# Picking a pair's tokens out of x by one-hot products in the last experts

## The reference

```python
def expert_choice_ffn(h, w_router, w_gate, w_up, w_down):      # h: 512 x 1024, 16 experts
    cap = CAPACITY_FACTOR * seq // N_EXPERTS                   # 64
    probs = softmax(h @ w_router)
    gate, idx = lax.top_k(transpose(probs), cap)               # each expert chooses its 64 tokens
    xs = h[idx]                                                # 16 x 64 x 1024
    a = xs @ w_gate[e]; u = xs @ w_up[e]                       # 1024 x 2048 each
    y = (silu(a) * u) @ w_down[e] * gate                       # 2048 x 1024
    return segment_sum(y, idx)                                 # added up by token

h2 = rms_norm_2(x, norm2_g)
x = x + expert_choice_ffn(h2, w_router, w_gate, w_up, w_down)
return rms_norm_2(x, final_g)
```

## Time and profile before

| what | us |
|---|---|
| median of 3 runs | 1988.26 (1986.86 to 1988.77) |
| profiled execution, its own time | 1970.76 |
| span of its trace, first to last instruction | 1969.4 |
| PE busy in the span | 1794.5 (91%) |
| DVE busy | 632.2 (32%) |
| ACT busy | 269.0 (14%) |
| POOL busy | 59.6 (3%) |

### The profile page before, as it was taken

How to read it: one execution, slowest core, us unless ns; L and a number is a source line. 1 busy time by engine, 2 the same in 40 slices (tenths; PEclk the granted TensorE clock), 3 DMA queues, 4 the chain that set the end, 5 groups by cost and what they waited for, 6 DMA issues and landing times.

```text
span 1969.4 us, 20545 instructions
## 1 busy us (share of the span) xinstructions
PE 1794.5 (91%) x8838; PEld 854.9 (43%) x8838; DVE 632.2 (32%) x1173; ACT 269.0 (14%) x490; POOL 59.6 (3%) x72
## 2 busy tenths in 40 slices
PE   8999999989999899999989999888888888888886
PEld 4778786533333354577554333222222222232222
DVE  7885453451213267954240111011111011111012
ACT  1251000210000155131010000000000000000001
POOL 0000000042100010000000000000000000000000
PEclk9999999989999999999999999999999999999999
DMA  8412226279999823013659999999999999999996
GB/s 230 146 43 82 90 86 243 101 247 418 425 425 410 307 99 115 25 60 125 267 203 365 427 428 426 429 427 429 427 428 427 428 428 427 428 427 429 427 428 266
DMA packets 88160, 593.04 MB, mean 301 GB/s; under 512 B 24832, under 2 KB 26240, under 8 KB 56832
## 3 DMA queue, kind: packets, MB, share of 16 engines
q1 hardware_dynamic: 79360, 563.24, 69.9%
q0 software_dynamic: 4544, 14.68, 2.1%
q10 hardware_dynamic: 4160, 13.75, 1.8%
HBM read 579.06 MB, written 12.59 MB: 300 GB/s over the span
## 4 chain that ended last, share of the span: by engine, by line
PE 59%; DMA 34%; DVE 4%; issue 1%; ACT 1%; POOL 0%; DVEq 0%; ACTq 0%; SPq 0%
PE ps L253 23%; DMA AR<-in_w_up 15%; PE ps L1399 10%; DMA ring<-in_w_up 7%; DMA AR<-in_w_down 7%; PE ps L2582 7%; PE ps L2608 6%; PE ps L2221 3%; PE ps L827 3%; DMA ring<-in_exp_w_gate 2%; DMA ring<-in_w_down 2%; PE ps L741 2%; PE ps L2116 1%; PE ps L267 1%; PE ps L2563 1%
## 5 line engine op out<-in xcount | busy, mean ns | idle before, releaser
L2722 DVE TENSOR_TENSOR XT<-XT,ps 128x512 f32<-128x512 f32 x128 | 82.0, 684 | 784.1 <-PE ps L2563 784.1
L253 PE MATMUL ps<-AR,ring 128*128 128x256 f32 (+1 forms) x904 | 275.3, 457 | 2.5 <-DVE AR L2412 2.4
L2582 PE MATMUL ps<-ring,AR 128*64 128x512 f32 x1008 | 229.3, 598 | 47.9 <-DMA ring<-in_w_up 31.0
L2582 PE MATMUL ps<-AR 128*64 128x512 f32 x1040 | 235.8, 597 | 31.5 <-DMA AR<-in_w_up 24.7
L1399 PE MATMUL ps<-ring,AR 128*32 128x512 f32 x1536 | 246.7, 593 | 6.1 <-DMA ring<-in_exp_w_gate 4.2
L253 PEld LDWEIGHTS ps<-AR,ring 128*128 128x128 f32 x904 | 171.1, 190 | 96.6 <-issue 77.4
L2582 PEld LDWEIGHTS ps<-ring,AR 128*64 128x64 f32 x1008 | 69.2, 136 | 200.4 <-issue 113.2
L2582 PEld LDWEIGHTS ps<-AR 128*64 128x64 f32 x1040 | 71.9, 137 | 191.5 <-issue 121.2
L253 PE MATMUL ps<-AR 128*128 128x256 f32 (+6 forms) x600 | 123.2, 353 | 7.8 <-DVE AR L1226 3.3
L1399 PE MATMUL ps<-AR 128*32 128x512 f32 x768 | 123.4, 593 | 0.0
L2608 PE MATMUL ps<-ring,AR 128*64 128x512 f32 x496 | 118.4, 626 | 4.7 <-DMA ring<-in_w_down 2.5
(11 more groups left out here) (383 smaller groups left out, 1458.0 us busy)
## 6 DMA issues: line engine op xcount, KB each, us to landing
AR<-in_w_gate SPq DMA_DIRECT2D x33, 2048.0 KB, 35.0
AR<-in_w_down SPq DMA_DIRECT2D x33, 2048.0 KB, 35.4
ring<-in_w_up SPq DMA_DIRECT2D x32, 2048.0 KB, 35.4
AR<-in_w_up SPq DMA_DIRECT2D x32, 2048.0 KB, 35.4
ring<-in_w_gate SPq DMA_DIRECT2D x31, 2048.0 KB, 32.1
ring<-in_w_down SPq DMA_DIRECT2D x31, 2048.0 KB, 35.4
ring<-in_exp_w_gate SPq DMA_DIRECT2D x15, 2048.0 KB, 11.8
ring<-in_w_in SPq DMA_DIRECT2D x14, 2048.0 KB, 10.0
```

Of the source, the lines that this page charges most:

```text
L253: x = PE.matmul(ps, l, r, start=i == 0, stop=i == len(pairs) - 1)
L2582: x = PE.matmul(GU[2 * m + f // 2][64 * (f % 2):64 * (f % 2) + 64, :], XS[n // 2 % 2][:, k * P + 64 * b:k * P + 64 * b + 64], w[:, kk_, f ...
L2722: DV.tensor_tensor(XK[:, o:o + T], XK[:, o:o + T], co_bank(i)[:, :], ALU.add).then_inc(d_co, 1)
```

## The change

- H2E, its four writes, the scaling of the rows (dve_turn splits, dve_rows stays with the first block only), the gathers, pool_choice, the index search and the index columns go.
- The choice keeps only the gate values of the two lists, and takes the 64th largest as the expert's threshold. PE spreads it to all partitions. DVE marks scores above it and equal to it, PE counts the marks by bf16 products with a triangle and with ones, and DVE makes of that a place (slots, 1 to 64, or 0) for each token and expert. Equal scores come behind the larger ones, in the order of tokens.
- For each pair DVE makes a one-hot matrix PICK of 512 tokens by 128 places, each row times the token's reciprocal root (sel). PE multiplies x with it: 8 blocks of 128 columns by 4 blocks of 128 tokens, 32 products of 128x128x128 (picks), and DVE multiplies the result with the norm's gain on its way to XS (gained). The gain (g22d) is loaded as columns.
- The pair's picks are done in the down phase of the pair before, behind its c = 1 and c = 2; those of pair 0 ahead of expert 0 and between its first products.
- cGE comes from one-hots of 128 tokens by 64 places for each block (gates, four operations of DVE), turned by four transposes in the down phase and copied from PSUM by DVE.
- x has to stay as it is until the last picks, so the results are added up in YS (4096 columns), and YS is added to x at expert 14.
- XS, cHE, cHB, cYE and cGE are single.
- The first eleven loads have the buffers 3, 2, 6, 7, 8, 4, 0, 10, 5, 1, 9, then nine go round: 3, 2, 6, 7, 8, 4, 0, 5, 1.

```diff
-        slot += [3, 2, 6, 7, 8, 0, 4, 5, 1, 9, 10]
-        slot += [(3, 2, 6, 7, 8, 0, 1, 9)[i % 8] for i in range(len(loads) - n_ec - 11)]
+        slot += [3, 2, 6, 7, 8, 4, 0, 10, 5, 1, 9]
+        slot += [(3, 2, 6, 7, 8, 4, 0, 5, 1)[i % 9] for i in range(len(loads) - n_ec - 11)]
...
+            SP.wait_ge(s_pp, 182)
+            for n in range(n1, n1 + NX + 1):
                 sp_load(n)
-            sp_load(n_ec + 6)
+            sp_load(n_ec + 7)
 
...
-            for a in range(4):
-                x = PE.transpose(Y5[1 - a // 2][0:16, sl(a % 2, P)], lg[:, a, :], ident)
+            for i in range(2):
+                x = PE.transpose(Y5[1][0:48, sl(i, P)], lg[:, 16 * i:16 * i + 48], ident)
             x.then_inc(s_cp, 1)
-            idle_products(DN, 14)
-
+            idle_products(DN, 11)
+            PE.wait_ge(s_cv, V2_TH)
+            PE.transpose(bank[3][:, 0:16], last_[0:16, 0:1].to_broadcast([16, P]), ident[0:16, 0:16]).then_inc(s_cp, 1)
+            idle_products(DN, 1)
+
+            PE.wait_ge(s_cv, V2_MK)
+            pos = bank[2][:, 0:128].rearrange("p (a n) -> p a n", a=4)
+            for t in range(4):
+                PE.matmul(pos[:, t, :], tri2, marks[:, t, :], start=t == 0, stop=False, skip_group_check=True)
+                if t < 3:
+                    PE.matmul(pos[:, t + 1:4, :], one2, marks[:, t:t + 1, :].to_broadcast([P, 3 - t, 32]), start=False,
+                              stop=False, skip_group_check=True)
+                x = PE.matmul(pos[:, :, 16:32], one2, marks[:, t:t + 1, 0:16].to_broadcast([P, 4, 16]), start=False,
+                              stop=t == 3, skip_group_check=True)
             x.then_inc(s_cp, 1)
+            idle_products(DN, 3)
...
+            def picks(k0, k1, ps):
+
+                for k in range(k0, k1):
+                    c = 256 * (k // 2) + k % 2
+                    x = matmuls(ps[:, sl(k - k0, P)], [(XT[:, a * D + c:a * D + c + 255:2],
+                                                        PICK[:, a, :, :].rearrange("p h s -> p (h s)")) for a in range(4)])
+                x.then_inc(e_tx, 1)
...
-            PE.wait_ge(s_cv, V2_ID)
-            idle_products(DN, 7)
-            rows(0)
+            PE.wait_ge(d_sel, 1)
+            for h in range(2):
+                picks(2 * h, 2 * h + 2, P_BANK[h])
             for n in range(16):
+                s0 = n % 2 * 64
...
+                        if n == 0 and m == 0:
+                            PE.wait_ge(d_xs, c + 1)
+                        elif c == 0 and m == 0:
+                            PE.wait_ge(d_xs, picked(n // 2))
+                            PE.wait_ge(d_he, 2 * n)
...
-                    if c == 1 and (n == 1 or b == 0 and 0 < n < 14):
-                        rows(n // 2 + 1)
+                    elif c < 2:
+                        picks(4 + 2 * c, 6 + 2 * c, P_BANK[2 + c])
...
+                    if c == 0:
+
+                        PE.wait_ge(d_gs, n + 1)
+                        transposes(TR, [GS[:, a, :, :].rearrange("p h s -> p (h s)") for a in range(4)]).then_inc(e_gt, 1)
+                    elif c < 3 and s0 and n < 15:
+                        if c == 1:
+                            PE.wait_ge(d_ge, n + 1)
+                            PE.wait_ge(d_sel, n // 2 + 2)
+                        picks(4 * c - 4, 4 * c, HB[c - 1])
...
+            src = Y5[1]
             for n in range(8):
                 g8 = gat[0:48, sl(n, 8)]
                 DV.max(g8, src[0:48, 0:256]).then_inc(s_dv, dv())
                 DV.wait_ge(s_dv, dv.n)
-                DV.max_index(ixu[0:48, sl(n, 8)].bitcast(U32), g8, src[0:48, 0:256]).then_inc(s_dv, dv())
                 if n < 7:
-                    DV.match_replace(wk[0:48, 0:256], g8, src[0:48, 0:256], -1.0).then_inc(s_dv, dv())
-                DV.wait_ge(s_dv, dv.n)
+                    op(DV.match_replace(wk[0:48, 0:256], g8, src[0:48, 0:256], -1.0))
                 src = wk
...
+            ga_, gb_ = gat[0:16, :], gatb[0:16, :]
+            op(DV.tensor_copy(gb_, gat[32:48, ::-1]))
+            op(DV.tensor_tensor(ga_, ga_, gb_, ALU.max))
+            DV.tensor_reduce(last_[0:16, :], ga_, AX.X, ALU.min).then_inc(s_cv, 1)
+            DV.wait_ge(s_cp, P2_TH)
+            th16 = bank[3][:, 0:16].unsqueeze(1).to_broadcast([P, 4, 16])
+            DV.tensor_tensor(marks[:, :, 0:16], scores, th16, ALU.is_gt)
+            DV.tensor_tensor(marks[:, :, 16:32], scores, th16, ALU.is_equal).then_inc(s_cv, 1)
+            DV.wait_ge(s_cp, P2_PS)
+            DV.wait_ge(s_cv, V2_MK)
+            op(DV.tensor_tensor(places_, bank[2][:, 0:128].rearrange("p (a n) -> p a n", a=4), marks, ALU.mult))
+            op(DV.tensor_tensor(slots, places_[:, :, 0:16], places_[:, :, 16:32], ALU.add))
+            io = cc("iota128")[:, 1:65]
+
+            def sel(j):
+
+                at_p = slots[:, :, 2 * j:2 * j + 2].unsqueeze(3).to_broadcast([P, 4, 2, 64])
+                op(DV.tensor_tensor(PICK, io.unsqueeze(1).unsqueeze(1).to_broadcast([P, 4, 2, 64]), at_p, ALU.is_equal))
+                flat = ones_at.rearrange("p (a s) -> p a s", a=4)
+                DV.tensor_tensor(flat, flat, ss.unsqueeze(2).to_broadcast([P, 4, P]), ALU.mult).then_inc(d_sel, 1)
+
+            def gates(n):
+
+                if n:
+                    DV.wait_ge(e_gt, n)
+                for a in range(4):
+                    x = DV.tensor_scalar(GS[:, a, :, :], io.unsqueeze(1).to_broadcast([P, 2, 64]), slots[:, a, n:n + 1],
+                                         scores[:, a, n:n + 1], ALU.is_equal, ALU.mult)
+                x.then_inc(d_gs, 1)
+
+            def gained(k0, k1, ps, tx):
+
+                DV.wait_ge(e_tx, tx)
+                DV.tensor_tensor(XS[:, k0:k1, :], ps[:, 0:P * (k1 - k0)].rearrange("p (k s) -> p k s", s=P),
+                                 g22d[:, k0:k1].unsqueeze(2).to_broadcast([P, k1 - k0, P]), ALU.mult).then_inc(d_xs, 1)
...
+                    if n == 0:
+                        DV.tensor_copy(YS[:, o:o + T], co_bank(i)[:, :]).then_inc(d_co, 1)
+                        continue
+                    DV.wait_ge(*((d_y, a + 1) if n == 14 else (d_co, i - 7)))
+                    y = (YS if n < 14 else XK)[:, o:o + T]
+                    DV.tensor_tensor(y, y, co_bank(i)[:, :], ALU.add).then_inc(d_co, 1)
...
+            sel(0)
+            DV.wait_ge(s_pn, 32)
+            for q in range(4):
+                gained(2 * q, 2 * q + 2, P_BANK[q], q + 1)
             for n in range(16):
-                DV.tensor_scalar(cGE[b], tau2, idd[:, n:n + 1], gts[:, n:n + 1], ALU.is_equal, ALU.mult).then_inc(d_ge, 1)
+                gates(n)
...
+                DV.wait_ge(e_gt, n + 1)
+                if n:
+                    DV.wait_ge(e_co, 8 * n)
+                DV.tensor_copy(cGE, TR[:, :]).then_inc(d_ge, 1)
+                if n % 2 and n < 15:
+                    sel(n // 2 + 1)
+                    for h in range(2):
+                        gained(4 * h, 4 * h + 4, HB[h], picked(n // 2) + h + 1)
+                if n == 14:
+                    DV.wait_ge(e_tx, picked(7))
+                    for a in range(4):
+                        DV.wait_ge(d_co, 8 * 13 + 2 * a + 2)
+                        DV.tensor_tensor(XK[:, sl(a, D)], XK[:, sl(a, D)], YS[:, sl(a, D)], ALU.add).then_inc(d_y, 1)
...
-        def pool_choice():
-            PO.wait_ge(s_cv, V2_LG)
-                PO.indirect_dma_start(XG2[j % 2], None, H2E, bass.IndirectOffsetOnAxis(idp[:, j:j + 1].bitcast(U32), 0))\
-                    .then_inc(s_xe[j % 2], 16)
-
         def sp_choice():
-            sp_load(n_ec + 5)
+            sp_load(n_ec + 6)
+
+            SP.wait_ge(b_o, 8)
             sp_load(n_ec + 8)
-
-            SP.wait_ge(b_o, 8)
-            sp_load(n_ec + 7)
+            sp_load(n_ec + 9)
             SP.wait_ge(s_cp, P2_LG)
-            sp_load(n_ec + 9)
-            SP.wait_ge(s_xe[0], 16)
             for n in range(n_ec + 10, len(loads)):
                 sp_load(n)
```

More of the change, by code:

```diff
@@ L104, in build @@
         GAINS = nc.dram_tensor("gain_rows", [1, 2 * D], F32, kind="Internal").ap()
-        H2E = nc.dram_tensor("h2_rows_2", [T, D], F32, kind="Internal").ap()
         YD = nc.dram_tensor("y_rows", [16 * FEW, D], F32, kind="Internal").ap()
@@ L2491, in build @@
-        tau2 = area(512)
-        XG2, XS = [area(D), XG2_1], [area(D), XS_1]
-        HK = [XG2[0], XS[0]]
-        gatb, ixb, first_ = (scr[:, 256 + 64 * i:320 + 64 * i] for i in range(3))
-        area = Area(h0)
-        cHE = [area(1024) for _ in range(2)]
-        cHB = [area(1024).rearrange("p (f t) -> p f t", t=64) for _ in range(2)]
+        slots, g22d = area(64).rearrange("p (a n) -> p a n", a=4), area(8)
+        JK = area(D)
+        XS = JK.rearrange("p (k s) -> p k s", k=8)
+        ones_at = area(512)
@@ new lines, in build @@
+        PICK, GS = (ones_at.rearrange("p (a h s) -> p a h s", a=4, h=2) for _ in range(2))
+        cYE, cGE = area(512), area(512)
```

(39 more changed lines are left out.)

175 lines of the change are left out of this document (53 added, 122 removed).

## The result

| | median us | runs | ratio to before, 95% interval |
|---|---|---|---|
| before | 1987.61 | 4 | |
| after | 1973.97 (1969.57 to 1976.59) | 4 | 0.9937 (0.9916 to 0.9957) |
| after, again | 1973.52 (1969.74 to 1975.10) | 6 | 0.9934 (0.9912 to 0.9955) |

In the later runs before has a median of 1986.0 to 1986.3 us, each with its own values beside those of the experiments. The change takes 12.4 to 13.6 us; 14.8 was forecast, to 1973.5 us.

The account below looks back on a forecast made before the run. The last experts' weight stream, 384.00 MB at 428 GB/s, was taken as the bound. Start -5.2, bytes -8.6 and buffers -1.0 gave -14.8 us, from 1988.26 to 1973.5 us; forecast 1971 to 1976 (0.62), range 1968 to 1982.

Parts of the forecast that it names:

- Start of expert 0: Choice ahead of the last experts: PE starts expert 0 at 1035.3 in place of 1040.52 us, 5.2 us earlier.
- Bytes: Last experts' stream: the gathers of pairs 1 to 7 go, 3.67 MB at 428 GB/s, worth 8.6 us.
- Buffers: Weight loads around expert 0: nine buffers close the 1.5 us hole, a later one of about 0.5 us appears; worth 1 us.
- The sign that I had named: Check for holes in the stream: no slice under 400 GB/s near 35 us after the start of expert 0.
- PE in the steady part: Expert pairs: net +6.3 us of PE work per pair, 109.7 against 117.6 us of stream; cost 0 while PE has slack.
- its fourth term: The steady part of the expert pairs: picks' cost on PE would show from about 11 us per pair, 0.17 per record.
- rival C: Steady part: PE becomes the bound at 0.278 us per pick record, 43 us slower, near 2032 us; chance 0.05.
- Tail: After the last load lands: gate transposes add 0.69 us in front, still hidden; change 0.
- Rival A: Choice before expert 0: the start is not gained, picks and placement replace the gather's wait; about 1979 us; chance 0.13.
- B: Weight stream: the gathers' bytes are worth little as packets interleave; -6.2 us, 1982 us; chance 0.07.
- D: Whole stage: start 7 us earlier, both holes gone (2.4), 9 for the gathers; -18.4 us, 1970 us; chance 0.10.
- E: Something earlier binds, for instance a late load holding PE's first products, so the ends cancel; 1988 us; chance 0.03.

Follow-up runs that it names:

- after, again: Changed kernel, no edit, measured again: 1973.52 us over 6 runs, ratio to before 0.9934.
- the first two profiles of before: Kernel before, unchanged, two profiled executions: spans 1969.4 and 1980.5 us, expert 0 at + 92.0 and + 90.3 us from the first w_out product of the second mixer.
- the third and fourth: Kernel before, unchanged, two more profiled executions: 1983.55 and 1984.91 us, expert 0 at + 94.8 and + 94.9 us from the second mixer's first w_out product.
- a quarter of the picks: Changed kernel, picks of pairs 1 to 7 adding up one of four blocks of 128 tokens (wrong output): 1972.5 us, ratio to before 0.9934.
- the doubled picks: Changed kernel, picks of pairs 1 to 7 done twice with the same result: 2000.95 us, ratio to before 1.0075.
- eight idle products: Changed kernel with 8 idle products in place of 11 ahead of the threshold: 1973.07 us, ratio to before 0.9934.
- eight buffers: Changed kernel with eight weight buffers going round in place of nine, slot 5 used once: 1978.12 us, ratio to before 0.9958.
- the bytes put back: Changed kernel with the 512 KB gain rows loaded again at experts 3 to 9, 3.67 MB in all: 1982.64 us, ratio to before 0.9982.

## Why the prediction was right

Forecast 1973.5 us, measured 1973.97 and 1973.52. The mechanism is right: a stream of fixed bytes that starts earlier and carries less. That the number is met within 0.5 us is in part luck. The change itself is 12.4 to 13.6 us and not 14.8; the median from which the forecast was counted, 1988.26 us of three runs, is 0.7 to 2.3 above every later one of before. And the profiled execution whose rows the terms were read from was not a typical one. Of the five terms the bytes hold, the start came out by an error and a gain that was not seen, the buffers and the tail lost time instead of gaining or keeping it, and the steady part cost next to nothing, as said, on a sum that is somewhat too small.

- **Start of expert 0** (5.2 us earlier). Against the first two profiles of before it is 1.3 to 3.3 us, against the third and fourth 5.8 to 6.2. My 5.2 was worked out against an execution whose idle products ran at the full level. After the change I had 35.3 - 17.6 = 17.7 us of choice, and the profiles show 18.2 and 19.6: picks at 0.124 a record in place of 0.11, and in one the threshold behind idle products. So I was 0.5 to 1.9 us short there. What made it up, by luck, was a gain that I had not seen: many executions of the kernel before hold expert 0 by the seven idle products at the lower level, 2.8 us in the choice (25.7 and 25.8 against 22.9), and in the changed kernel the same effect costs at most the 1.75 us at the threshold. That the start passes through to the end is shown.
- **Bytes** (8.6 us). Shown from both sides: 3.15 MB taken from the kernel before give 7.2 us, 3.67 MB put back after the change cost 9.1. Per MB that is 2.3 and 2.5 us (2.0 by the profile of the second), where 428 GB/s is 2.3.
  The page rule that I weighed, software-generated descriptors slowing two DMA engines (the Trainium skill, DMA: Bandwidth & Descriptors, Latency and other measured facts), is not borne out: the software queue's bytes gave no more than the hardware queue's cost. What the DMA engines 7 and 15 did by themselves no view here shows. The 358 GB/s of the Trainium skill (DMA: Bandwidth & Descriptors, Where 436 GB/s comes from) did not bind here either: this one core read 380 MB at 427.
- **Buffers** (1 us gained). Failed in sign. From expert 0 on, the bytes missing at 428 GB/s in stretches under full rate are 2.4 to 2.6 us before, and 4.3 to 4.7 after (without the end): some 2 us lost. The hole did not close, it moved and grew: 301 GB/s at + 35 became 351 to 403 from + 39 to + 59. My sum had the first release of the down phase at + 37.6, and it came at + 38.7, and the next ones came one at a time. The sign that I had named, no stretch under 400 GB/s near + 35, failed in this way. "From then on the ninth buffer is worth nothing" is wrong as well: without it the time is 4.6 us longer.
- **PE in the steady part** (0). Right in what counts: the stream runs at 427 to 428 GB/s, and with a quarter of the picks the time is only 1.0 us less. The sum of a pair is met by the first one only, 108.9 us against 109.7. The next pairs, while PE does not yet wait for the stream, take 109 to 112 us, because down products run at the lower level of the clock in some of them (5.35 in place of 3.65 us), which no term of mine had. The forecast gives two points where the picks would decide, about 11 us per pair in its fourth term and 12.7 in rival C. With 15.5 us of them, the doubled picks, the kernel is 14.7 us slower than before. Seven pairs with a straight line through that put the point at 15.5 - 14.7 / 7 = 13.4 us, as an estimate, and the pair of 119.5 us less the 15.5 leaves 117.6 - 104.0 = 13.6 us of room. So 12.7 was near.
- **Tail** (0). About 1 to 2 us lost. Counted as if the last bytes had all come at 428 GB/s, they end 23.1 to 23.5 us ahead of the span's end in the four profiles of before, and 25.4 and 24.4 in the two of the changed kernel. The down products at the lower level add to it (5.35 and 4.44 us for the first 16 records; before has 3.65 in the first profile and 4.91 in the third); the gate transposes and c = 1 to 3 behind them leave PE no pause. With eight idle products, where the holes are larger, it is 23.3: a stream that ends later hides the tail, so the two are not separate losses.

Together by the profiles: expert 0 to end 4.6 us less (8.6 of bytes, less some 2 of holes and 1 to 2 of tail), and 6.0 in the start, 10.6 in all against the third and fourth profile of before, and 8.4 and 6.1 against the first and second. The medians say 12.4. The remaining 2 us are not settled. The mark lies equally early in both kernels' profiles but for the first, and single executions scatter by 10 us or more. One thing bears on it: the third and fourth profile of before, at 1983.55 and 1984.91 us, are themselves shorter than its median. Among its runs the 14 with a mean granted clock of 0.976 or less have a median of 1988.4 us, and the 12 with 0.981 or more one of 1981.8; no execution at 0.976 was profiled.

Rival A (start not gained) is refuted by the table of starts, with the smallest gain at 1.3 us; B (bytes worth little) by the two experiments on them; C's mechanism, PE as the bound, exists and lies beyond 13 us of picks per pair, and its price of 0.278 us per record did not occur (3.97 us for 32); D overstates; E did not occur.

## What to carry to other kernels

When a stage waits for a stream of fixed bytes, count three things alone: the start of the stream's refill, the bytes in it, the holes. Here the start reached the end one to one, the bytes nearly so, and the holes in part, since work that PE has left behind the last bytes hides some of them. Lay a mark where the code is the same before two profiles are compared, and profile the old kernel more than once: the first profile here was 11 to 13 us ahead of the other three of its kernel at the mark, and 3 us shorter than two of them inside the choice. A forecast that is met by a sum of terms of which two are off is met partly by luck; only runs that move one term each show which. Work that fills a wait to keep the clock up is itself on the path when the clock falls.

## What the hardware showed unexpectedly

- The fill products cost 4.78 or 7.24 us for 14 records, by the level of the clock at which they happened to run (1.00, or 0.50 for the first 5 us), behind an equal idle time of 2.7 us.
- An fp32 product of 128x128x128 takes 0.25 us in a row, weights included (3.97 us for 16 products, which are 32 records), with the weights read from x at a stride of two.
- The mark's place varies in code that both kernels share. Between 424 and 459 us PE had gaps of up to 1.1 us for which the profile shows no cause in the second and third profile of before, in both of the changed kernel, with eight buffers and with the bytes put back, and none in the first of before. Their cause was not tried, and that they account for the whole difference is not shown.
